# Latent attention: both halves of the probabilities scaled on GpSimd, the score scale in the copy of the queries

## The reference

```
def mla_attention(cq, ckv, kr, gq, gkv, wuq, wukv, cos, sin):
    q = (rmsnorm(cq, gq) @ wuq).reshape(B_, S, D_HEADS, D_NOPE + D_ROPE)
    q = jnp.concatenate([q[..., :D_NOPE], apply_rope(q[..., D_NOPE:], cos, sin)], axis=-1)
    ...
    return blocked_attention(q, k, v, (D_NOPE + D_ROPE) ** -0.5)

def block(qi):                                   # in blocked_attention
    s = jnp.einsum('bqhd,bkhd->bhqk', qi, k).astype(jnp.float32) * scale
    p = jax.nn.softmax(s, axis=-1)
    return jnp.einsum('bhqk,bkhe->bqhe', p.astype(v.dtype), v)
```

## Time and profile before

| | |
|---|---|
| median of 3 runs | 2061.62 us (2060.53 to 2062.73) |
| the profiled execution, its span | 2062.5 us; no other time of it is given |
| busy: PE, DVE, ACT, POOL | 95%, 48%, 34%, 16% |
| in the stage, 1600 to 1634 us: PE, DVE, ACT, POOL | 29.44, 30.84, 22.15, 9.86 us of 34 |

### The profile page before, as it was taken

One profiled execution on the slowest core, in us unless ns is written; L12 is line 12 of the kernel. 1 busy time (PEld: TensorE's weight loads), 2 busy tenths in 40 slices (PEclk: granted clock), 3 DMA queues, 4 the chain that ended last, 5 costly groups with the idle time before them and its releaser, 6 DMA issues.

```text
span 2062.5 us, 23191 instructions
## 1 busy us (share of the span) xinstructions
PE 1952.7 (95%) x8888; PEld 1592.7 (77%) x8888; DVE 997.9 (48%) x1058; ACT 706.1 (34%) x932; POOL 334.4 (16%) x274
## 2 busy tenths in 40 slices
PE   6999999997989999999999999999948999999997
PEld 4888888785868888888878888887726778888885
DVE  6334421668778533342163343216988753433223
ACT  4222221436346422221142222214746542222212
POOL 2111100213113211110021111002345221111001
PEclk9999999998989999999999999999979999999998
DMA  4222222221211222222222222222210022222221
GB/s 148 99 102 100 83 102 102 96 78 37 82 42 42 92 92 102 102 88 95 102 82 102 102 93 90 102 102 90 82 41 21 22 82 102 94 89 102 102 102 41
DMA packets 36211, 176.66 MB, mean 86 GB/s; under 512 B 12752, under 2 KB 13136, under 8 KB 15552
## 3 DMA queue, kind: packets, MB, share of 16 engines
q1 hardware_dynamic: 33696, 172.55, 24.1%
q10 hardware_dynamic: 2304, 2.98, 0.4%
q0 software_dynamic: 160, 0.43, 0.1%
HBM read 173.85 MB, written 2.10 MB: 85 GB/s over the span
## 4 chain that ended last, share of the span: by engine, by line
PE 83%; DVE 8%; ACT 4%; POOL 2%; issue 2%; ACTq 0%; DMA 0%; POOLq 0%; DVEq 0%
PE ps L264 27%; PE ps L266 27%; PE ps L265 27%; POOL acc L333 2%; DVE xgl L299 1%; DVE eD L1180 1%; ACT eD L1135 1%; DVE small L1164 1%; DVE wl L234 1%; ACT wh L230 1%; DVE small L679 1%; DVE th L1755 1%; ACT eA L687 0%; PE ps L862 0%; DVE x L289 0%
## 5 line engine op out<-in xcount | busy, mean ns | idle before, releaser
L264 PE MATMUL ps<-xgh,wh 128*128 128x512 f32 x1792 | 709.9, 396 | 27.7 <-DVE xgl L299 25.4
L265 PE MATMUL ps<-xgl,wh 128*128 128x512 f32 x1792 | 698.8, 390 | 0.0
L266 PE MATMUL ps<-xgh,wl 128*128 128x512 f32 x1792 | 698.8, 390 | 0.0
L234 DVE TENSOR_TENSOR wl<-raw,wh 128x2048 fp32r<-128x2048 f32 (+1 forms) x157 | 360.3, 2295 | 541.1 <-ACT wh L230 541.0
L230 ACT ACTIVATE wh<-raw 128x2048 fp32r<-128x2048 f32 (+1 forms) x157 | 297.9, 1897 | 384.1 <-PE ps L266 382.8
L264 PEld LDWEIGHTS ps<-xgh,wh 128*128 128x128 f32 x1792 | 336.9, 188 | 110.9 <-DVE xgl L299 19.2
L265 PEld LDWEIGHTS ps<-xgl,wh 128*128 128x128 f32 x1792 | 337.0, 188 | 71.0 <-issue 3.4
L266 PEld LDWEIGHTS ps<-xgh,wl 128*128 128x128 f32 x1792 | 336.8, 188 | 71.1
L264 PE MATMUL ps<-ah,wh 128*128 (+1 forms) x704 | 273.9, 389 | 0.0
L265 PE MATMUL ps<-al,wh 128*128 (+1 forms) x704 | 273.9, 389 | 0.0
L266 PE MATMUL ps<-ah,wl 128*128 (+1 forms) x704 | 273.9, 389 | 0.0
(11 more groups left out here) (243 smaller groups left out, 1573.9 us busy)
## 6 DMA issues: line engine op xcount, KB each, us to landing
raw<-in_units SPq DMA_DIRECT2D x161, 1024.0 KB, 4.7
x<-in_xT ACTq DMA_DIRECT2D x8, 256.0 KB, 6.0
outT<-x SPq DMA_DIRECT2D x8, 256.0 KB, 2.1
relb<-in_rpb SPq DMA_DIRECT2D x64, 24.0 KB, 2.1
cosA<-in_rope_a ACTq DMA_DIRECT2D x1, 256.0 KB, 2.7
sinA<-in_rope_a ACTq DMA_DIRECT2D x1, 256.0 KB, 2.9
cosD<-in_rope_d POOLq DMA_DIRECT2D x1, 192.0 KB, 3.0
sinD<-in_rope_d POOLq DMA_DIRECT2D x1, 192.0 KB, 2.7
```

Of the source, the lines that this page charges most:

```text
L234: nc.vector.tensor_tensor(wl[:, c % 2, 0:n], raw[:, c % 2, 0:n], wh[:, c % 2, 0:n].bitcast(F32), ALU.subtract).then_inc(w_lo, 1)
L264: nc.tensor.matmul(dst, lh, rh, start=first, stop=False)
L265: nc.tensor.matmul(dst, lh, rl, start=False, stop=False)
L266: return nc.tensor.matmul(dst, ll, rh, start=False, stop=last)
```

## The change

Five edits belong together. The scale MS moves from the exponential (and from the bias) into the ACT copy of the projected queries, so the scores come out of PE scaled; the keys' copy is left as it is. The row maximum is then written negated by the reduction itself, and the small multiplication L1166 is gone with its semaphore `mxraw`. DVE no longer scales tile 0: POOL scales both tiles, tile 0 first, each announced on one semaphore `m_norm`, and its quarter of the weight split follows the second. PE's transposes wait for the one semaphore. The reciprocal of step j still waits until POOL has scaled step j - 2.

```
--- before.py
+++ after.py
@@ -579,7 +579,6 @@
         kr_lo = sem("kr_lo")
         vd_hi = sem("vd_hi")
         vd_lo = sem("vd_lo")
-        mxraw = sem("mxraw")
         setup_act_done = sem("setup_act_done")
 
         STEP_SEMS = ("scores", "max", "exp", "rec", "turned", "hi", "lo", "pv")
@@ -588,7 +587,6 @@
         n_norm = sem("n_norm")
         n_norm2 = sem("n_norm2")
         m_norm = sem("m_norm")
-        m_norm2 = sem("m_norm2")
 
 
 
@@ -1100,10 +1098,7 @@
                         pe.wait_ge(kr_lo, 8)
                     for t in range(2):
                         z = 2 * j + t
-                        if t == 0:
-                            pe.wait_ge(m_norm, j + 1)
-                        else:
-                            pe.wait_ge(m_norm2, j + 1)
+                        pe.wait_ge(m_norm, z + 1)
                         if z >= 3:
                             pe.wait_ge(SM["lo"], z - 2)
                         for k in range(TT):
@@ -1133,7 +1128,7 @@
             for t in range(2):
                 c = 2 * (i % 2) + t
                 nc.scalar.activation(eD[:, i % 2, t, :], ps[:, mla_bank(i) + t, :], ACT.Exp, bias=col(C_NMX + c),
-                                     scale=MS, accum_out=col(C_SUM + c)).then_inc(SM["exp"], 1)
+                                     accum_out=col(C_SUM + c)).then_inc(SM["exp"], 1)
 
         def mla_act(act):
             for i in range(20):
@@ -1161,10 +1156,8 @@
         def mla_max_dve(dve, i):
             b = 2 * (i % 2)
             dve.wait_ge(SM["scores"], 2 * i + 2)
-            nc.vector.tensor_reduce(col(C_CF + b, 2), ps[:, mla_bank(i):mla_bank(i) + 2, :], AX, ALU.max).then_inc(mxraw, 1)
-            dve.wait_ge(mxraw, i + 1)
-            nc.vector.tensor_scalar(col(C_NMX + b, 2), col(C_CF + b, 2), -MS, None,
-                                    ALU.mult).then_inc(SM["max"], 1)
+            nc.vector.tensor_reduce(col(C_NMX + b, 2), ps[:, mla_bank(i):mla_bank(i) + 2, :], AX, ALU.max,
+                                    negate=True).then_inc(SM["max"], 1)
 
         def mla_dve(dve):
             for i in range(18):
@@ -1173,12 +1166,8 @@
                     rec = recs[:, 2 * (j % 2):2 * (j % 2) + 2]
                     dve.wait_ge(SM["exp"], 2 * j + 2)
                     if j >= 2:
-                        dve.wait_ge(m_norm2, j - 1)
-                        dve.wait_ge(m_norm, j - 1)
+                        dve.wait_ge(m_norm, 2 * (j - 1))
                     nc.vector.reciprocal(rec, col(C_SUM + 2 * (j % 2), 2)).then_inc(SM["rec"], 1)
-                    dve.wait_ge(SM["rec"], j + 1)
-                    nc.vector.tensor_scalar(eD[:, j % 2, 0, :], eD[:, j % 2, 0, :], rec[:, 0:1], None,
-                                            ALU.mult).then_inc(m_norm, 1)
                 if 1 <= i < 16:
                     mla_max_dve(dve, i)
                 j = i - 2
@@ -1195,9 +1184,10 @@
             pool.wait_ge(kr_lo, 8)
             for j in range(16):
                 pool.wait_ge(SM["rec"], j + 1)
-                nc.gpsimd.tensor_tensor(eD[:, j % 2, 1, :], eD[:, j % 2, 1, :],
-                                        recs[:, 2 * (j % 2) + 1:2 * (j % 2) + 2].broadcast_to([P, SEQ]),
-                                        ALU.mult).then_inc(m_norm2, 1)
+                for t in range(2):
+                    rec = recs[:, 2 * (j % 2) + t:2 * (j % 2) + t + 1]
+                    nc.gpsimd.tensor_tensor(eD[:, j % 2, t, :], eD[:, j % 2, t, :], rec.broadcast_to([P, SEQ]),
+                                            ALU.mult).then_inc(m_norm, 1)
                 if 1 <= j < 9:
                     split_lo_part(pool, U_WO + (j - 1) // 4, (j - 1) % 4, 2 + (j - 1) // 4)
 
@@ -1639,7 +1629,8 @@
                     if i >= 2:
                         act.wait_ge(qdc_done, i - 1)
                         act.wait_ge(rotd_done, i - 1)
-                    nc.scalar.activation(qd32[:, i % 2, :], ps[0:96, (i - 1) % 2, :], ACT.Copy).then_inc(qd32_done, 1)
+                    nc.scalar.activation(qd32[:, i % 2, :], ps[0:96, (i - 1) % 2, :], ACT.Copy,
+                                         scale=MS).then_inc(qd32_done, 1)
                 h = i - 1
                 if 0 <= h < 8:
                     act.wait_ge(kd_ps, h + 1) if h < 7 else act.wait_ge(w_half, 2 * (U_UKV + 1))
```

## The result

The changed kernel takes 2047.93 us (median of 4 runs, 2047.22 to 2048.65), the kernel before 2061.07 us (4 runs, 2059.53 to 2062.73): a ratio of 0.993, interval 0.9916 to 0.9944, 13.1 us faster. The prediction gave 8.7 us (2052.9, range 2050.8 to 2057.2).

What follows compares the result with a forecast made beforehand. It took the DVE-ACT loop, 4.42 us a step, as the bound, then PE at 3.85. Gains of 9.3 less 0.2 gave 9.1, taken as 8.7; median 2061.62 less 8.7 is 2052.9 us, range 2050.8 to 2057.2.

Steps and rivals of the forecast that it cites:

- (f): Steady steps of the attention stage: PE becomes the bound at 3.85 us a step against 4.42; all other waits fit.
- (h): Stage end: 14th output product twelve steps of 3.85 after the second, at 1624.6, 9.3 us earlier; 0.2 given back after.
- (a): DVE's scaling L1180 goes from the DVE-ACT loop: 1.29 us less a step, not 0.48.
- (b): L1166 goes because the maximum is written negated: maximum to exponential 1.30 us instead of 1.45, 0.15 less a step.
- (d): POOL scales both halves, 1.00 to 1.04 us each; its step is 3.47 with the weight split, 2.04 without.
- (c): Scale moved into ACT's query copy and out of the exponential: no time change, 0; 0.8 us kept as an end.
- (e): The DVE-ACT loop after the change: 0.20 + 1.30 + 1.48 = 2.98 us a step.
- (g): Stage start: step 1's reciprocal 0.28 us earlier; second output product at 1578.4 instead of 1581.41, 3.0 gained.
- POOL as bound: Rival: POOL scalings of 1.29 or 1.47 us make POOL the bound; 7.1 or 4.2 us gained; chance 0.10.
- The wait for oD: Rival: PE keeps waiting for ACT's copy of oD, step 4.25 us, only 3 us gained (2058.6); chance 0.06.
- The slower one: Rival: POOL's two scalings hold DVE's maximum, loop 5.02 us, 9 us slower (2070.6); chance 0.04.

Runs made afterwards that it cites:

- e2_scale_only: Changed kernel with DVE scaling tile 0 again and POOL only tile 1, leaving the moved scale and negated maximum: 2058.80 us, 0.9986 of the kernel before.
- e1_pool_only: Changed kernel with the scale back in exponential and bias and the small multiplication back; POOL still scales both halves: 2054.74 us, 0.9968 of the kernel before.
- e3_pe_less: Changed kernel without the third matmul of each output product (8 matmuls in place of 12): 2042.76 us, 0.9907 of the kernel before.
- e4_pool_more: Changed kernel with a third POOL scaling in each step, into a scratch tile nobody reads: 2054.95 us, 0.9965 of the kernel before.
- e5_first_max_later: Changed kernel with DVE's first maximum behind the last rotation and ACT's high query part ahead of the first exponentials: 2049.58 us, 0.9944 of the kernel before.
- e7_keys_first: Changed kernel with the low part of the last head's keys moved on DVE ahead of the first maximum: 2047.59 us, 0.993 of the kernel before.
- c3_after: Changed kernel as it is, run a third time for another trace: 2048.50 us, 0.9942 of the kernel before.
- c2_after: Changed kernel as it is, run again for a second trace: 2047.34 us, 0.9937 of the kernel before.

## Why the prediction was wrong in size

The sum forecast 9.1 us, shaded to 8.7; the stage and lead gave 12.8. What failed is the count of PE's work: its step in (f), 3.85 us for 3.70 measured, and the number of full steps in (h), twelve for eleven and a short one. Point by point:

- *What bounds the kernel; (a).* Right. The loop of DVE and ACT was the step. e2_scale_only, which keeps DVE's scaling, stays at 4.22.
- *(b) Near in the old neighbourhood, wrong for its worth.* With DVE scaling it is worth 0.20 a step (e2_scale_only), 0.15 forecast. But part (d) makes POOL busy just when L1166 would come, and L1166 would have taken 0.72 to 0.99 instead of 0.17 (e1_pool_only). I priced (b) beside the old POOL. The sum was not hurt, since it had L1166 out, but its split between the parts would have been: without (b) the gain is 8.4 of 12.8, not nearly all.
- *(c).* Right, nothing to see: the exponentials take 0.69 as before.
- *(d).* Right: 1.04 each, 1.00 apart. The split behind them took 1.29, not 1.47: beside L1180 it took 1.47 (in e2_scale_only, too), and L1180 is gone. POOL's step is 3.25 to 3.3.
- *(e).* The loop without waits is 2.83 (the trace of after, reciprocals at 1568.30, 1571.13 and 1573.96), 2.98 forecast. ACT has no idle time in these steps either, so 2.83 is its own step there, too. The shorter loop told only at the start, in (g).
- *(f) The step that was mis-sized.* PE is the bound, as e3_pe_less shows. But its step is 1.51 + 1.39 + 0.80 = 3.70 (1597.01, 1598.52, 1599.91, 1600.71), not 3.85. The 0.94 for transposes to output product came from the earlier trace rows, where the transposes follow an output product; there their first record starts only 0.12 after the last matmul, behind scores 0.23. A distance between starts was taken out of one neighbourhood into another; the case with 1.04 in its place, which gave 3.95 and 7.9 us, lay further off. Eleven steps: 1.65 us.
- *(g).* The second output product comes 12.23 after the first scores; forecast 1578.4 - 1565.69 = 12.71. 0.5 us. The reciprocal of step 1 came as forecast, 5.71 behind the first scores (5.72); the exponentials of step 3 came 9.86 behind them, 0.45 earlier than forecast, and the copy of oD, taken for the last to come, was in time: ACT works its first steps back to back at 2.8.
- *(h) The count that failed.* It has 12 steps of 3.85 from the second to the 14th output product. But iteration 16 has no scores, so its step has 1.39 less work: 2.72 measured (1615.51 to 1618.23), in which transposes to output product take 1.21 and not 0.80, since PE waits for oD there. Before, the slower loop had hidden that: the earlier trace rows give 4.37 in the mean over all twelve. This is 1.1 us, and the end after it was 0.3 better than forecast.
- 1.65 + 0.5 + 1.1 + 0.3 + 0.15 (the lead: 0.25 for 0.10) = 3.7, which with 9.1 is the 12.8. The shading by 0.4 went the wrong way. The medians, 13.1 us apart, agree with the 12.8 within their scatter.
- *The rivals.* POOL as bound didn't come, but e4_pool_more shows it was near. The wait for oD vanished but for 0.2 once. The slower one was half true: POOL's scalings do hold a DVE instruction, the one that the change removes; they don't hold the maximum or the subtraction.
- *The range.* Its low end, 2050.8, is 10.8 gained: the best case of the prediction's own rows (9.8) and 1.0 below it, where its text says half a us. It has no term for a count being off. Its high end, 2057.2, leaves the POOL case at 2057.4 just outside, which the text says it takes in.

The profiled span of before was also no good base for fractions of a per cent: over the 12 traces, whose work up to there is all but the same, the scores of step 0 begin within 4.8 us.

## What to carry to other kernels

When a loop's bound moves to another engine, work out that engine's step anew from its own instruction list, iteration by iteration; the last iterations lack parts, and the old bound hid it. Count an edit's worth next to the other edits and not next to the old neighbours: a two-element tensor_scalar on DVE took 0.17 us beside an idle GpSimd and 0.72 to 0.99, to the end of the running scaling, beside a busy one; a reduction with a negated result did it in 0.155. Folding it away cost nothing that shows: the copy of the queries with the scale takes 0.60, as without it. And compare stretches of a trace, which repeated within hundredths (once 0.6 us off), before comparing spans that scatter by microseconds.

## What the runs showed that I had not expected

- A tensor_scalar over 128 x 2 float32 elements in SBUF ended only with the running GpSimd scaling (e1_pool_only): 934 ns in the median against 169 in the mean of the kernel before; a reduction over the same elements beside the same work takes 155.
- The hold seems to go both ways: GpSimd's split quarter took 1469 ns in the mean beside the end of DVE's scaling (1468 in e2_scale_only, which has it, too) and 1288 without it (1290 in e1_pool_only).
- In e5_first_max_later and e7_keys_first, with 3.4 and 1.6 us of idle time on PE ahead of the scores, these still ran at the full clock, and it was down only behind them.
- The half clock at the stage's start ended 5.4 us after the first scores (1562.59) in the first trace of the changed kernel and 6.9 us after them (1560.90) in c3_after, with the same instructions and the same idle time (4.08) ahead; in c2_after it was 4.7 us. The windows of PE of the one,

```profile
1566.00:1567.00 1.00, 1.00 (x3) 0.50 0.00 0
1567.00:1568.00 1.00, 1.00 (x4) 0.51 0.00 0
1568.00:1569.00 1.00, 1.00 (x10) 1.00 0.00 0
```

and of the other:

```profile
1567.00:1568.00 1.00, 1.00 (x6) 0.58 0.00 0
1568.00:1569.00 1.00, 1.00 (x6) 1.00 0.00 0
```

What decides between them no run here shows.
